# Loading a relative position bias as one run of 157 floats per query row and head

## What is computed

```python
dc = col_idx - cols[:, None] + (WIN_W - 1)
...
dr = rs + jnp.arange(kh) - r + (WIN_H - 1)
bias = rpb[:, dr[None, :, None], dc[:, None, :]]
logits = jnp.einsum('bqhd,bkqwhd->bhqkw', q_r, k_r).astype(jnp.float32) * scale
logits = logits + bias.astype(jnp.float32)[None]
```

## Time and profile before

| | |
|---|---|
| median of 3 runs | 1120.6 us (1119.57 to 1121.55) |
| the profiled execution | 1121.41 us |
| its span in the trace | 1119.5 us (1.9 us lie around it) |
| PE, DVE, ACT, POOL busy | 91%, 75%, 40%, 40% of the span |
| packets of GpSimd's DMA queue | 37888, 2.25 MB, 10.8% of 16 engines |
| packets of SP's DMA queue | 109264, 208.58 MB, 59.3% of 16 engines |

### The profile page before, as it was taken

One profiled execution on the slowest core, in us unless ns is written; L12 is line 12 of the kernel. 1 busy time (PEld: TensorE's weight loads), 2 busy tenths in 40 slices (PEclk: granted clock), 3 DMA queues, 4 the chain that ended last, 5 costly groups with the idle time before them and its releaser, 6 DMA issues.

```text
span 1119.5 us, 20306 instructions
## 1 busy us (share of the span) xinstructions
PE 1022.4 (91%) x6766; PEld 937.1 (84%) x6766; DVE 836.6 (75%) x1474; ACT 449.9 (40%) x645; POOL 447.0 (40%) x310
## 2 busy tenths in 40 slices
PE   6599999799999999999999999109999999999995
PEld 5577898699999999999999999107888888888884
DVE  3247547667999999888888888007888888888887
ACT  4155544334343434444444444003444444444442
POOL 6700000004888888888888888860000000000000
PEclk9799999899999999999999999658999999999998
DMA  9766489662666665977777775227878787777773
GB/s 258 189 225 226 172 271 302 222 237 58 144 139 134 149 131 139 200 172 171 169 164 176 168 169 106 1 27 247 240 241 238 245 240 242 241 241 240 244 238 131
DMA packets 147183, 211.22 MB, mean 189 GB/s; under 512 B 47696, under 2 KB 95568, under 8 KB 147152
## 3 DMA queue, kind: packets, MB, share of 16 engines
q1 hardware_dynamic: 109264, 208.58, 59.3%
q0 software_dynamic: 37888, 2.25, 10.8%
HBM read 192.81 MB, written 17.96 MB: 188 GB/s over the span
## 4 chain that ended last, share of the span: by engine, by line
PE 45%; POOL 36%; issue 8%; DVE 5%; DMA 4%; ACT 1%; POOLq 0%; DVEq 0%; SPq 0%; ACTq 0%
POOL expert_weights L440 36%; PE ps L1231 31%; PE ps L1156 12%; DMA w_raw<-in_w_in_dram 3%; DVE w_lo L868 1%; ACT w_hi L548 1%; PE ps L1054 1%; PE ps L1032 1%; DMA xres<-in_x_dram 1%; DVE xres L668 0%; DVE xres L675 0%; PE ps L1004 0%; PE ps L1042 0%; DMA expert_weights<-gw,cell 0%; DVE small L656 0%
## 5 line engine op out<-in xcount | busy, mean ns | idle before, releaser
L440 POOL DMA_INDIRECT expert_weights<-gw,cell x256 | 407.6, 1592 | 287.3 <-DVE gw L861 208.5
L1189 PE MATMUL ps<-act_hi,uT_hi 128*128 128x256 f32 x1024 | 295.2, 288 | 0.4 <-DVE uT_lo L929 0.4
L1189 PE MATMUL ps<-act_hi,uT_lo 128*128 128x256 f32 x1024 | 289.9, 283 | 0.0
L1189 PE MATMUL ps<-act_lo,uT_hi 128*128 128x256 f32 x1024 | 289.7, 283 | 0.0
L622 ACT ACTIVATE v_hi<-v_raw 128x512 fp32r<-128x512 f32 x256 | 147.8, 625 | 255.5 <-PE ps L1231 200.0
L1231 PE MATMUL ps<-v_hi,hid_hi 128*128 128x512 f32 x512 | 158.8, 391 | 54.2 <-DVE v_lo L948 54.2
L1189 PEld LDWEIGHTS ps<-act_hi,uT_hi 128*128 128x128 f32 x1024 | 196.6, 192 | 0.6 <-issue 0.6
L1189 PEld LDWEIGHTS ps<-act_lo,uT_hi 128*128 128x128 f32 x1024 | 196.6, 192 | 0.0
L1189 PEld LDWEIGHTS ps<-act_hi,uT_lo 128*128 128x128 f32 x1024 | 196.3, 192 | 0.0
L948 DVE TENSOR_TENSOR v_lo<-v_raw,v_hi 128x512 fp32r<-128x512 f32 x256 | 164.9, 685 | 0.0
L1231 PEld LDWEIGHTS ps<-v_hi,hid_hi 128*128 128x128 f32 x512 | 96.6, 189 | 74.8 <-issue 54.7
(11 more groups left out here) (147 smaller groups left out, 1417.2 us busy)
## 6 DMA issues: line engine op xcount, KB each, us to landing
v_raw<-in_peer_v_dram SPq DMA_DIRECT2D x128, 512.0 KB, 4.2
u_raw<-in_peer_u_dram SPq DMA_DIRECT2D x68, 512.0 KB
u_raw<-in_peer_u_dram SPq DMA_DIRECT2D x240, 128.0 KB
w_raw<-in_w_in_dram SPq DMA_DIRECT2D x8, 2048.0 KB, 9.3
expert_weights<-zeros SPq DMA_DIRECT2D x16, 1024.0 KB, 12.4
g_in<-expert_weights SPq DMA_DIRECT2D x128, 128.0 KB, 3.1
w_raw<-in_peer_wq_dram SPq DMA_DIRECT2D x4, 2048.0 KB, 11.0
w_raw<-in_w_out_dram SPq DMA_DIRECT2D x2, 2048.0 KB, 9.1
```

The lines of the kernel that those rows point to most:

```text
L440: pool.indirect_dma_start(out=table_cells, out_offset=bass.IndirectOffsetOnAxis(ap=cell[:, t, k:k + 1], axis=0), in_=gw[:, t, k:k + 1], in ...
L1189: ins = pe.matmul(ps[:, bank, 0:T], (uT_hi, uT_hi, uT_lo)[part][:, slot, k, :], (act_hi, act_lo, act_hi)[part][:, k, :], start=(k == 0 and ...
```

## The change

Before, each of 32 transfers reads, for each query column and key row, 64 floats. The four runs of one query and head overlap or touch in the table: together they are 3 x 31 + 64 = 157 neighbouring floats. After, there are 12 transfers (three groups x 4 query rows), each over all heads of its group, which read these 157 floats as one run of 628 B into a new tile `bias_raw`. GpSimd's `affine_select` then reads its rows out of `bias_raw`, 31 floats apart, and writes the masked `bias`: for each half of the partitions and each key row one select for columns 16 to 63 and one for columns 0 to 15 (8 together), and one more in place for columns 16 to 47, where both sides of the window matter. That is 9 for each half of the partitions, 18 for each group, 54 in all, where there were 12. GpSimd waits for `mask_done` once before each ninth select. DVE waits for 18 counts a group in place of 4.

```diff
+BIAS_RUN = (ROWS - 1) * RPB_W + GRID_W
...
+    bias_raw = sb("bias_raw", [P, HEADS, TB, BIAS_RUN], 185 * K1)
...
         def load_bias(group):
-            for h in range(*BIAS_HEADS[group]):
-                for r in range(ROWS):
-                    at = (h * RPB_H + WIN_H - ROWS + r) * RPB_W + WIN_W - GRID_W
-                    src = bass.AP(na_rpb.tensor, na_rpb.offset + at,
-                                  [[1, GRID_W], [RPB_W, ROWS], [1, GRID_W]])
-                    b, p0 = r // 2, GRID_W * (r % 2)
-                    dst = bias[p0:p0 + GRID_W, h, b, :].rearrange("p (r c) -> p r c", r=ROWS)
-                    pool.dma_start(dst, src).then_inc(s[f"rpb_in{group}"], 16)
+
+            h0, h1 = BIAS_HEADS[group]
+            for r in range(ROWS):
+                at = (h0 * RPB_H + WIN_H - ROWS + r) * RPB_W + WIN_W - GRID_W
+                src = bass.AP(na_rpb.tensor, na_rpb.offset + at,
+                              [[1, GRID_W], [RPB_H * RPB_W, h1 - h0], [1, BIAS_RUN]])
+                b, p0 = r // 2, GRID_W * (r % 2)
+                pool.dma_start(bias_raw[p0:p0 + GRID_W, h0:h1, b, :], src).then_inc(s[f"rpb_in{group}"], 16)
...
-            pool.wait_ge(s[f"rpb_in{g}"], 16 * ROWS * (heads[1] - heads[0]))
-            for c0, base, sign in masks:
-                for p0 in (0, GRID_W):
-                    if done:
-
-                        pool.wait_ge(s["mask_done"], done)
-                    part = bias[p0:p0 + GRID_W, heads[0]:heads[1]] \
-                        .rearrange("p h b (r c) -> p (h b r) c", c=GRID_W)[:, :, c0:c0 + GRID_W - WIN_W]
...
+            pool.wait_ge(s[f"rpb_in{g}"], 16 * ROWS)
+            pairs = (heads[1] - heads[0]) * TB
+            for p0 in (0, GRID_W):
+                whole = bias[p0:p0 + GRID_W, heads[0]:heads[1]].rearrange("p h b (r c) -> p (h b) r c", c=GRID_W)
+                (c1, base1, sign1), (_, base2, sign2) = masks
+                for r in range(ROWS):
+                    for c0, c, base, sign in ((c1, GRID_W - c1, base1, sign1), (0, c1, base2, sign2)):
+                        run = free(bias_raw[p0:p0 + GRID_W, heads[0], 0, :], (BIAS_RUN, pairs), (1, c),
+                                   start=r * RPB_W + c0)
+                        pool.affine_select(out=whole[:, :, r, c0:c0 + c], in_=run, compare_op=ALU.is_ge, fill=MASKED,
+                                           base=base, pattern=[[0, pairs], [sign, c]],
+                                           channel_multiplier=sign).then_inc(s["mask_done"], 1)
+                        done += 1
+
+                pool.wait_ge(s["mask_done"], done)
...
+                pool.affine_select(out=both, in_=both, compare_op=ALU.is_ge, fill=MASKED, base=base2 + c1 * sign2,
+                                   pattern=[[0, pairs * ROWS], [sign2, GRID_W - WIN_W - c1]],
+                                   channel_multiplier=sign2).then_inc(s["mask_done"], 1)
```

More of the change, by code:

```diff
@@ new lines, in _ @@
+            pairs = (heads[1] - heads[0]) * TB
[11 more added lines that the diff above has]
+                pool.wait_ge(s["mask_done"], done)
+                both = bias[p0:p0 + GRID_W, heads[0]:heads[1]] \
+                    .rearrange("p h b (r c) -> p (h b r) c", c=GRID_W)[:, :, c1:GRID_W - WIN_W]
+                pool.affine_select(out=both, in_=both, compare_op=ALU.is_ge, fill=MASKED, base=base2 + c1 * sign2,
+                                   pattern=[[0, pairs * ROWS], [sign2, GRID_W - WIN_W - c1]],
+                                   channel_multiplier=sign2).then_inc(s["mask_done"], 1)
+                done += 1
@@ L680, in logits @@
             dve.wait_ge(s["score_done"], h + 1)
-            dve.wait_ge(s["mask_done"], 4 * (1 + [g for g, r in enumerate(BIAS_HEADS) if r[0] <= h < r[1]][0]))
+            dve.wait_ge(s["mask_done"], 2 * (2 * ROWS + 1) * (1 + [g for g, r in enumerate(BIAS_HEADS) if r[0] <= h < r[1]][0]))
             if h >= 2:
```

## The result

The kernel after the change takes 1106.44 us (median of 4 runs, 1105.84 to 1107.59), the kernel before 1120.18 us beside it: a ratio of 0.9877, with a 95% interval from 0.986 to 0.9894, 13.7 us less. Measured a second time, both on one chip again, it was 1105.57 against 1121.3 us, 0.9869 (0.9851 to 0.9888). The ratios are given as recorded, with their intervals; they are not always the quotient of the two medians. The forecast was 1110.5 us and a range from 1106.5 to 1118.0. The direction was right, and so was the wait that shrinks.

What follows compares the result with a forecast made beforehand. The prediction took TensorE's wait for chunk v's weights, delayed by the bias transfers, as the bound. It took 10.1 us of saved DMA time from the median of 1120.6, other terms at 0, giving 1110.5 us, range 1106.5 to 1118.0.

Steps and rivals of the forecast that it cites:

- The bound: Start of the kernel: TensorE idles 11.22 us for chunk v's weights, delayed by bias transfers; a microsecond gained there reaches the end.
- The term of the transfers: GpSimd's bias loads: DMA time falls from 16.1 to 6.0 us, a gain of 10.1 us (6.2 to 12.1).
- How a descriptor splits into AXI transactions: Bias loads: runs starting off a 256 B boundary fetch extra bytes; 8.0 us of DMA time left, 8.1 gained.
- Specifications: Bias loads: 628 B runs, over the 512 B minimum, move at the weights' rate; 3.3 us left, 12.8 gained.
- What the gain does to chunk v: Chunk v's load: lands at 36.1 us, not 46.2, so TensorE begins v 10.1 us earlier, at 41.2.
- The cap: TensorE's gap before chunk v: 11.2 us is the most that it holds.
- The clock: TensorE at chunk v: the low clock after the gap may go, 0 to 2 us; taken as 0.
- Issuing, masking, collision: GpSimd: issues end at 19.0 us; 21.6 us of masking, hidden, ends near 45; collision with DVE costs 0, at most 1.6.
- (c): Chunk v's load: its last packet waits in a slow ring the bias doesn't load, so no gain, 1120.6 us; chance 0.08.
- (b): Gain partly eaten by sv staying put, k landing late or dearer runs: 2.2 to 6.2 us gained; chance 0.13.
- (d): Bias loads: 16 engines read the same few hundred bytes; 30.2 us of DMA time, slower, 1134.7 us; chance 0.08.

Runs made afterwards that it cites:

- mask_only: The kernel before with its old 32 bias transfers, masked in place by the 54 selects of after; 1121.36 us, ratio 1.0005.
- no_bias: The kernel before with a memset of zeros in place of the 32 bias transfers; 1105.35 us, ratio 0.9869.
- short_runs: The kernel after with each run of 157 floats cut into four of 39 or 40, 8192 runs in 48 transfers; 1106.27 us, ratio 0.9875.
- sv_later: The kernel before, with SP issuing chunk sv only when chunk v has landed; 1118.96 us, ratio 0.9978.
- heads_together: The kernel before with its 8192 runs shared out over 48 transfers, each of one query row, one key row and all heads of a group; 1114.94 us, ratio 0.9932.
- paced: The kernel before with a memset of 0.5 us and a wait for it between GpSimd's 32 issues; 1129.6 us, ratio 1.0078.

## Why the prediction was right or wrong

**The bound.** Right. The wait for chunk v was what the transfers cost, and mask_only and no_bias put the whole gain on them.

**The term of the transfers.** 10.1 us of DMA time were forecast, 10.9 measured (16.1 to 5.2). The sum was nearly right, by luck, on a wrong split. It gave each run 20.8 ns of its own and 0.041 ns a byte; the runs show 5.8 ns and 0.0555 ns a byte, and for the kernel before another 11 ns, because a transfer's reads lie in one place. At 628 B the two splits happen to lie near each other (46.7 against 40.6 ns). Had the change cut the runs instead, the same working would have missed by a factor of two, as the expectation of short_runs did.

The Trainium skill ("DMA: Bandwidth & Descriptors") was drawn on with two sections, and neither estimate was met: "How a descriptor splits into AXI transactions" led to 8.0 us left and "Specifications", with its 512 B, to 3.3; 5.2 were measured. The line through 157, 628 and 896 B has no step at 512 B. The rule on beats failed by what it was scaled from. By it, runs at every float offset take 9.3, 24.0 and 32.4 beats on average for 157, 628 and 896 B; scaled from the measured 40.6 ns at 628 B, an estimate from that page is 15.8 and 54.8 ns for the other two. The traces have 14.5 and 55.5, so among these three they agree with it to a tenth. The estimate of 8.0 us had started from the 31.4 ns of the kernel before, of which 11 are the price of the place.

**What the gain does to chunk v.** The step that failed. It said that v lands earlier by the DMA time saved, 36.1 us; it landed at 31.5. All DMA work between 16 and 46 us but the bias was taken to stay ahead of v. Part of it was chunk sv, issued at 34.19. By the queues, 3.9 us of SP's transfers left the stretch ahead of v's landing, and 10.9 + 3.9 = 14.8 against the 14.7 measured; sv_later, which holds only sv back, gives 2.8 to 3.5 us. The row stood in the prediction, in the rival (c), as a reason why nothing might come of the change. "The engines are full" was right; what they were full of was read wrongly.

**The cap.** "11.2 us is the most that this gap holds" is true of the gap and was taken for the most that chunk v can gain. It is not, as k itself came earlier, where the forecast had it the same or 1.6 us later: ACT had k at 20.37 us and not 22.59. Its first product moved from 26.88 to 25.7, and the low clock behind its gap, about 1.7 us, went with the gap. 11.2 + 1.2 + 1.7 = 14.1 us, which is what chunk v began earlier.

**The clock.** Taken at 0 of a possible 2 us. With the gap before v gone, the granted clock stays at 1.00, 2.4 GHz, through k and v, where before it fell twice. From the start of v to the first head's logits it took 18.5 us before and 16.7 after, 1.8 less. That the gap before k had brought the low clock was no reason to keep it: k came 2.2 us earlier, and of the 2.66 us gap nothing is left in this profile, in which chunk q ran at half pace at its start. In the second profile, with q at full pace, 1.09 us are left, and the granted clock stays at 1.00 there too.

**Issuing, masking, collision.** Right in that they cost nothing. 12 issues ended at 19.2 us for the forecast 19.0. Masking took 32 us, not 21.6, and ended at 52 us, not 45. The collision had been counted for DVE alone, but selects that run beside DVE are stretched (2.70 us for one that takes 0.72 alone). The last half group, with DVE idle but for its end, took 3.9 us as forecast. DVE's remainders of k and v took 2.29 to 2.58 us and delayed nothing. Head 0 came at 55.1 us and found group 0 ready since 28.3.

**The rivals.** (b) didn't happen, though heads_together shows that its mechanism is real: in the kernel after, sv lands 8.1 us after its issue, at 38.6, and ACT takes it up at 43.0. (c) said that nothing would come of it, and fell. Engines that have run out of work while v waits for others, which it rested on, are seen in sv_later; they take some of a gain and not all of it. (d) had seen the cause: the reads of one place, at 0.77 us a packet. It was given the wrong side, since the change itself cuts the number of reads of a place by four and lets a transfer read at two or three heads' places at once. The 30.2 us of the forecast were never met: the nearest is paced with 27.4, but with 8192 runs of 256 B where the forecast had 2048 of 628, at 53.5 ns a run and not 96; that the two totals are alike is chance.

**Open.** What in the memory or the fabric makes one place slow is not shown, only that it is the place. Nor is it known how much of the 40.6 ns of a 628 B run is still the price of the place, as no kernel reads such runs spread over a larger table; heads_together leaves 5 ns a run above the line without a cause. How sv holds up v within the engines is open too.

## What to carry to other kernels

When a small table is loaded many times over, look at the place that is read as well as at bytes and runs: 16 engines on the same few hundred bytes were up to 3.7 times as slow (53.5 against 14.6 ns a run) as the same runs read apart. In a full queue, list all that is ahead of the awaited load and all that shares the engines with it, the next load too, and ask of each whether the change lets it start later or earlier. A long gap that closes can give back the low clock behind it: here it was 1.7 us at k and 1.8 us at v. Put it in the sum, with the gaps that will be left.

## What the hardware showed that was not expected

GpSimd's issue of a transfer took 0.62 us for 128, 192 or 256 runs alike (12 in 7.50 us, 32 in 19.77, 48 in 28.99). Fewer transfers in flight made each of them dearer: 27.4 us of DMA time when paced, 16.1 when not, for the same bytes. And a load issued 18 us after another on the same queue, while that one was under way, made it land about 3 us later (2.8 to 3.5).
